# Group norm of an RWKV-7 time mix, taken head pair by head pair: centring product in PSUM, variance spread by a ones block, inverse root by logarithm and exponential

## What is computed

```python
y = tm(ys)                                   # 16 heads of 64
mean = jnp.mean(y, axis=-1, keepdims=True)
var = jnp.mean(jnp.square(y - mean), axis=-1, keepdims=True)
yn = ((y - mean) * lax.rsqrt(var + GN_EPS)).reshape(bsz, t_len, D_MODEL)
yn = yn * ln_w.astype(f32) + ln_b.astype(f32)
o = ((yn + bonus.reshape(bsz, t_len, D_MODEL)) * g.astype(f32)).astype(h.dtype)
return o @ w_o, ...
```

## Time and profile before

| | us |
|---|---|
| median of 3 runs | 1508.48 (1508.26 to 1512.67) |
| the profiled execution, its own time | 1510.38 |
| its span from the first to the last instruction | 1508.4 |
| PE busy in it | 1429.3 (95%) |
| DVE, ACT, POOL busy | 872.7, 565.6, 32.0 |
| group norm, first product to first product of `w_o` | from 611.7 to 641.0 |

### The profile page before, as it was taken

One profiled execution on the slowest core, in us unless ns is written; L12 is line 12 of the kernel. 1 busy time (PEld: TensorE's weight loads), 2 busy tenths in 40 slices (PEclk: granted clock), 3 DMA queues, 4 the chain that ended last, 5 costly groups with the idle time before them and its releaser, 6 DMA issues.

```text
span 1508.4 us, 28845 instructions
## 1 busy us (share of the span) xinstructions
PE 1429.3 (95%) x11934; PEld 1379.3 (91%) x11934; DVE 872.7 (58%) x1290; ACT 565.6 (37%) x724; POOL 32.0 (2%) x44
## 2 busy tenths in 40 slices
PE   4999999688799999899999999999999999999997
PEld 4999999577598998399999999999999999999997
DVE  5555544866995323676555546555556877655544
ACT  4333323385343320244333334334333235334332
POOL 0000000300001000100000000000000000000000
PEclk9999999898898995699999999999999999999998
DMA  4443344222244000124343444443344443444342
GB/s 190 158 146 141 114 135 163 90 86 92 60 146 134 11 17 33 53 85 167 139 141 139 135 165 145 142 155 139 131 139 157 155 153 124 155 158 148 124 154 94
DMA packets 44221, 189.00 MB, mean 125 GB/s; under 512 B 15888, under 2 KB 17296, under 8 KB 28016
## 3 DMA queue, kind: packets, MB, share of 16 engines
q1 hardware_dynamic: 44144, 187.89, 36.0%
HBM read 182.65 MB, written 5.22 MB: 125 GB/s over the span
## 4 chain that ended last, share of the span: by engine, by line
PE 86%; DVE 6%; ACT 4%; issue 3%; POOL 1%; DMA 1%; SPq 0%; DVEq 0%; ACTq 0%
PE psum L329 46%; PE psum L361 21%; PE psum L790 4%; PE psum L497 4%; ACT w_hi L242 1%; PE psum L968 1%; PE psum L1033 1%; PE psum L1020 1%; PE psum L1017 1%; PE psum L951 1%; PE psum L937 1%; PE psum L998 1%; PE psum L925 1%; DVE w_lo L247 1%; DVE rstd L318 1%
## 5 line engine op out<-in xcount | busy, mean ns | idle before, releaser
L329 PE MATMUL psum<-x_hi,w_hi 128*128 128x322 f32 (+2 forms) x1600 | 501.9, 314 | 22.8 <-DVE x_lo L294 17.8
L247 DVE TENSOR_TENSOR w_lo<-w_raw,w_hi 128x2048 fp32r<-128x2048 f32 (+1 forms) x188 | 388.6, 2067 | 226.4 <-ACT w_hi L242 226.0
L329 PE MATMUL psum<-x_lo,w_hi 128*128 128x322 f32 (+2 forms) x1600 | 501.3, 313 | 0.0
L329 PE MATMUL psum<-x_hi,w_lo 128*128 128x322 f32 (+2 forms) x1600 | 499.9, 312 | 0.0
L242 ACT ACTIVATE w_hi<-w_raw 128x2048 fp32r<-128x2048 f32 (+1 forms) x188 | 325.9, 1733 | 460.1 <-PE psum L329 229.2
L329 PEld LDWEIGHTS psum<-x_hi,w_hi 128*128 128x128 f32 x1600 | 302.6, 189 | 25.6 <-issue 21.5
L329 PEld LDWEIGHTS psum<-x_hi,w_lo 128*128 128x128 f32 x1600 | 303.5, 190 | 0.0
L329 PEld LDWEIGHTS psum<-x_lo,w_hi 128*128 128x128 f32 x1600 | 303.1, 189 | 0.3
L361 PE MATMUL psum<-h_hi,w_hi 128*128 128x322 f32 (+2 forms) x704 | 219.8, 312 | 0.0
L361 PE MATMUL psum<-h_lo,w_hi 128*128 128x322 f32 (+2 forms) x704 | 219.7, 312 | 0.0
L361 PE MATMUL psum<-h_hi,w_lo 128*128 128x322 f32 (+2 forms) x704 | 219.5, 312 | 0.0
(11 more groups left out here) (192 smaller groups left out, 1449.5 us busy)
## 6 DMA issues: line engine op xcount, KB each, us to landing
w_raw<-in_gu SPq DMA_DIRECT2D x88, 1024.0 KB, 4.8
w_raw<-in_down SPq DMA_DIRECT2D x64, 704.0 KB, 4.0
w_raw<-in_mix SPq DMA_DIRECT2D x16, 1024.0 KB, 4.8
w_raw<-in_scin SPq DMA_DIRECT2D x12, 1024.0 KB, 4.8
w_raw<-in_wo SPq DMA_DIRECT2D x4, 1024.0 KB, 4.9
w_raw<-in_scout SPq DMA_DIRECT2D x4, 1024.0 KB, 4.7
s<-in_wkv SPq DMA_DIRECT2D x8, 256.0 KB, 4.4
out_wkvs<-s SPq DMA_DIRECT2D x8, 256.0 KB, 2.0
```

The costliest lines, as they stand in the source:

```text
L247: dve.tensor_tensor(wlo[par][:, :n], raw[par][:, :n], whi[par][:, :n].bitcast(F32), ALU.subtract).then_inc(lo_ready, 1)
L329: last = pe.matmul(PS[:, banks[j], :n], w[:, (2 * k + j) * P:(2 * k + j + 1) * P], v[:, k, :n], start=(k == 0 and i == 0), stop=(k == KT - ...
```

## The change

The group norm is done pair by pair, with other operations:

- A matrix `centre` (one on the diagonal minus a 64th of the head's block of ones) is built once, on DVE, after the inverses. PE multiplies y by it (L890 of the new kernel; this is the centred y) into PSUM banks 4 to 7, and it stays there. DVE's subtraction is gone.
- ACT squares it out of PSUM. PE multiplies the squares by the block of ones into banks 2 and 3, so the sum stands on all 64 rows of the head: the pass that spread it is gone.
- ACT takes the logarithm of the variance plus epsilon, and then the exponential of minus one half of it: the inverse root. Square root and reciprocal are gone.
- DVE multiplies the centred y in PSUM by the inverse root in memory. DVE also writes the low part of the result, which POOL did.
- PE starts the group norm only when the last state and the last bonus have left banks 4 to 7 (`seq_ready`, `bonus_ready`). Before, its first two passes used banks 0, 1 and 6.
- `seq_stored` is split in two; DVE waits for the four stores whose memory it takes, SP for the other four before it loads slot 2 of `w_o`.

```diff
             pe.wait_ge(y_evac, CHUNKS)
-            for p in range(PAIRS):
+            pe.wait_ge(centre_ready, 1)
+            pe.wait_ge(seq_ready, SEQS)
+            pe.wait_ge(bonus_ready, PAIRS)
+
+            def centred(p):
+                if p >= 4:
+                    pe.wait_ge(gn_used, p - 3)
+                pe.matmul(PS[:, 4 + p % 4, :NY], centre[:, :], ar[:, 1, p, YC:], start=True, stop=True)\
+                    .then_inc(yc_ready, 1)
+
+            def variance(p):
+                pe.wait_ge(yc_sq, p + 1)
                 if p >= 2:
-                    pe.wait_ge(yc_ready, p - 1)
-                pe.matmul(PS[:, p % 2, :NY], con[:, K_BLOCK:K_BLOCK + P], ar[:, 1, p, YC:], start=True, stop=True)\
-                    .then_inc(mean_done, 1)
...
+                    pe.wait_ge(gn_log, p - 1)
+                pe.matmul(PS[:, 2 + p % 2, :NY], con[:, K_BLOCK:K_BLOCK + P], tmp[6 + p % 2][:, :NY],
+                          start=True, stop=True).then_inc(var_done, 1)
+
+            for p in range(4):
+                centred(p)
+            variance(0)
+            variance(1)
+            for p in range(2, PAIRS):
+                variance(p)
+                if p + 2 < PAIRS:
+                    centred(p + 2)
             project_pe(pe, "wo", 2, T - 14, 0)
...
+            def square(p):
                 act.wait_ge(yc_ready, p + 1)
                 if p >= 2:
                     act.wait_ge(var_done, p - 1)
-                act.activation(tmp[6 + p % 2][:, :NY], ar[:, 1, p, YC:], ACT.Square).then_inc(yc_sq, 1)
...
+                act.activation(tmp[6 + p % 2][:, :NY], PS[:, 4 + p % 4, :NY], ACT.Square).then_inc(yc_sq, 1)
+
+            def inverse_root(p):
+                root = (acc, ms)[p % 2][:, :NY]
+                act.wait_ge(var_done, p + 1)
+                if p >= 2:
+                    act.wait_ge(gn_used, p - 1)
+                act.activation(root, PS[:, 2 + p % 2, :NY], ACT.Ln, bias=GN_EPS, scale=1.0 / HD).then_inc(gn_log, 1)
+                act.wait_ge(gn_log, p + 1)
+                act.activation(root, root, ACT.Exp, scale=-0.5).then_inc(gn_inv, 1)
+
+            def take_o(p):
                 act.wait_ge(o_ready, p + 1)
                 act.activation(ohi[:, p, :NY], tmp[2 + p % 4][:, :NY], ACT.Copy).then_inc(ohi_ready, 1)
+
+            square(0)
+            square(1)
+            for p in range(PAIRS):
+                inverse_root(p)
+                if p + 2 < PAIRS:
+                    square(p + 2)
+                if p:
+                    take_o(p - 1)
+            take_o(PAIRS - 1)
             project_act(act, "wo", 2)
...
             inverses(dve, split)
+            link(dve, dve.tensor_scalar(centre[:, :], con[:, K_BLOCK:K_BLOCK + P], -1.0 / HD, None, ALU.mult))
+            for hh in range(2):
+                rows = slice(HD * hh, HD * hh + HD)
+                last = dve.tensor_tensor(centre[rows, rows], centre[rows, rows], con[rows, K_EYE:K_EYE + HD], ALU.add)
+            last.then_inc(centre_ready, 1)
             split(16)
             chain_dve(dve, split)
...
-                dve.tensor_tensor(t, PS[:, 4 + p % 2, :NY], ar[:, 1, p, YC:], ALU.mult).then_inc(gn_used, 1)
+                dve.wait_ge(gn_inv, p + 1)
+                dve.tensor_tensor(t, PS[:, 4 + p % 4, :NY], (acc, ms)[p % 2][:, :NY], ALU.mult).then_inc(gn_used, 1)
                 dve.wait_ge(gn_used, p + 1)
...
+                if p:
+                    low_o(p - 1)
+            low_o(PAIRS - 1)
             project_dve(dve, "wo", 2)
```

More of the change, by code:

```diff
@@ L146, in build_program @@
         one = at("one", [P, C], start=o4 + 4 * PAIRS * (PCHUNKS + SEQS) + 4 * T)
+        centre = at("centre", [P, P], start=o4 + 4 * PAIRS * (PCHUNKS + SEQS) + 4 * T + 4 * C)
         gt = [at("gt0", [P, C * C], start=iv), at("gt1", [P, C * C], start=e_start + 6 * 4 * TS)]
@@ L736, in build_program @@
         seq_ready = sem("seq_ready")
-        seq_stored = sem("seq_stored")
+        seq_stored = [sem(f"seq_stored{i}") for i in range(2)]
         final_stored = sem("final_stored")
@@ L881, in mix_pe @@
             pe.wait_ge(y_evac, CHUNKS)
[L882 to L896 removed]
+            pe.wait_ge(centre_ready, 1)
[8 more added lines that the diff above has]
+                pe.wait_ge(yc_sq, p + 1)
+                if p >= 2:
+                    pe.wait_ge(gn_log, p - 1)
[9 more added lines that the diff above has]
+                    centred(p + 2)
             project_pe(pe, "wo", 2, T - 14, 0)
[L899 removed]
+        centre_ready = sem("centre_ready")
         rk_spread = sem("rk_spread")
@@ L1275, in mix_pool @@
                 last.then_inc(arm_ready, 1)
-            for p in range(PAIRS):
-                pool.wait_ge(ohi_ready, p + 1)
-                pool.tensor_tensor(olo[:, p, :NY], tmp[2 + p % 4][:, :NY], ohi[:, p, :NY].bitcast(F32),
-                                   ALU.subtract).then_inc(olo_ready, 1)
         def inverses(dve, split):
@@ L1448, in mix_dve, with low_o @@
             inverses(dve, split)
+            link(dve, dve.tensor_scalar(centre[:, :], con[:, K_BLOCK:K_BLOCK + P], -1.0 / HD, None, ALU.mult))
[3 more added lines that the diff above has]
+            last.then_inc(centre_ready, 1)
             split(16)
             chain_dve(dve, split)
-            for p in range(PAIRS):
-                dve.wait_ge(mean_done, p + 1)
-                dve.scalar_tensor_tensor(out=ar[:, 1, p, YC:], in0=PS[:, p % 2, :NY], scalar=-1.0 / HD, in1=ar[:, 1, p, YC:],
-                                         op0=ALU.mult, op1=ALU.add).then_inc(yc_ready, 1)
-            dve.wait_ge(gn_root, 1)
-            dve.reciprocal(rstd[0:HEADS, :NY], ms[0:HEADS, :NY]).then_inc(gn_inv, 1)
-            dve.wait_ge(seq_stored, 16 * SEQS)
+            def low_o(p):
+                dve.wait_ge(ohi_ready, p + 1)
+                dve.tensor_tensor(olo[:, p, :NY], tmp[2 + p % 4][:, :NY], ohi[:, p, :NY].bitcast(F32),
+                                  ALU.subtract).then_inc(olo_ready, 1)
+            dve.wait_ge(seq_stored[0], 16 * SPC)
+            dve.wait_ge(bonus_ready, PAIRS)
             for p in range(PAIRS):
```

15 lines of the change are left out of this document (3 added, 12 removed).

## The result

| | before | after |
|---|---|---|
| median in one comparison | 1510.27 (6 runs, 1508.26 to 1512.83) | 1517.62 (6 runs, 1516.39 to 1522.87) |
| ratio after to before | | 1.0054, interval 1.0039 to 1.0069: +8.2 us (5.9 to 10.4) |
| profiled execution, its span | 1508.4 | 1514.4 |

The forecast of 1512.4 and its range to 1516.0 were both too low. The ratio and its interval are estimated from all runs of a comparison and are not the quotient of the medians, which lie 7.35 us apart. The kernel after was timed twice more, beside the experiments: 1.0055 (1.0037 to 1.0073) and 1.0052 (1.0033 to 1.0072). Slower it is: the medians of the three comparisons lie 7.35, 8.5 and 6.9 us apart.

The account below looks back on a forecast made before the run. PE was taken as the bound, waiting on the serial group norm, with ACT's table loads pacing the new one. The first projection slot's end moved from 649.39 to 653.35, so 1508.5 + 3.9 = 1512.4, range 1510.0 to 1516.0.

Parts of the forecast that it names:

- 1 PE's start: Group norm's first product on PE: waits for the last bonus, at 612.42 instead of 611.74, 0.7 us lost.
- 2, 3 first logarithm: Four centring products end at 616.7; with 1.2 us for the first variance product, ACT's first logarithm starts at 617.9.
- 4 first exponential: On ACT, logarithm 0.44 and table load 1.28 with small gaps: the first exponential starts at 619.65.
- 5 first to last exponential: ACT's pair loop with two table loads: five steps of 4.28 us and two of 3.92, together 29.2.
- 6 last gate operation ends: DVE's multiply, weight and bonus, bias and gate on the last pair: ends at 651.05.
- rival D: ACT's steps slightly shorter or the clock rising early: 0.3 us back in step 3, total 1512.1; within the forecast's width.
- rival B: Table loads cost nothing after the first: first projection slot 8.5 us earlier, total 1500.0; chance 0.05.
- rival C: Each table switch hides a 1.38 us drain on ACT: 20.7 us on top of 3.9, total 1533; chance 0.03.
- step 7: Projection's first slot: after the last low parts, PE's 12 products of tiles 6 and 7 take 1.8 us, ending at 653.35.
- Rival A: Clock falls after PE's pause before tile 6: 12 products take 3.3 us, slot end +5.4, total 1514.1; chance 0.30.
- everything behind it as before, shifted: After the projection's first slot, the program's end moves by as much as that slot's end, nothing added.
- same: Whole program within the 4.5 us (0.3%) that a measurement can tell, line at 1513.0; chance 0.51.

Follow-up runs that it names:

- b_exp: Kernel before plus a one-element exponential right after the group norm's square root; 1511.6, ratio 1.0006.
- b_wait: Kernel before plus the changed kernel's wait of PE for the last state and last bonus before the group norm; 1512.51, ratio 1.0008.
- a_sqrt: Changed kernel plus a one-element square root on ACT after the last high part; 1514.32, ratio 1.0025.
- a_copy: Changed kernel with the logarithm replaced by a copy, for timing only, the computed result being different; 1500.83, ratio 0.9939.
- a_fill_more: Changed kernel plus twelve unused products in PE's pause before tile 6 of the output projection, repeated in more rounds; 1515.86, ratio 1.0051.
- a_pool: Kernel of a_abs with the low parts moved from DVE back to POOL; 1496.10, ratio 0.9919.
- a_abs: Changed kernel with one inverse-root function for logarithm and exponential, plus a one-element square root after the last high part; 1495.24, ratio 0.9908.

## Why the prediction was wrong, point by point

The terms of the stage, counted from PE's first product in the forecast (612.42) and in the trace (609.98):

| step | forecast | measured |
|---|---|---|
| 1 PE's start, against before | +0.7 | +0.78 |
| 2, 3 first logarithm | 5.48 | 5.74 |
| 4 first exponential | 7.23 | 7.49 |
| 5 first to last exponential | 29.2 | 28.87 |
| 6 last gate operation ends | 38.63 | 38.61 |
| 7 tile 6 starts | 39.13 | 39.07 |
| 7 the 12 products of tiles 6 and 7 | 1.8 | 2.57 |

In the second execution of the kernel after everything from the first logarithm to tile 6 came 0.8 earlier (tile 6 at 38.30), in the third as in the table; rival D had said that the clock may rise early, and gave it 0.3.

**Right.** Every load took 1.28 and none was free (against rival B) or had anything hidden behind it (against rival C). The exponentials stand 4.22 apart for 4.28, since the high part starts 0.32 behind the square (630.15 to 630.47) where I took 0.36. DVE's gate operation took 0.55 to 0.56 throughout. DVE waited for ACT 1.8 to 2.2 us in a pair. `centre` took 0.22 + 0.45 on DVE ahead of a weight's low part, and the wait on `seq_stored` ended nothing: DVE's first multiplication was released by the exponential (the wait of 8.2 us for L1227, the longest).

```profile
464.08 0.22 DVE L1473 TENSOR_SCALAR centre<-con 128x128 f32<-128x128 f32 x1
464.34 0.45 DVE L1476 TENSOR_TENSOR centre<-centre,con 64x64 f32<-64x64 f32 x2
464.82 2.71 DVE L248 TENSOR_TENSOR w_lo<-w_raw,w_hi 128x2048 fp32r<-128x2048 f32 x1
```

**Wrong: step 7, "At 2.4 GHz they take 12 x 0.15".** Rival A was what happened, in all three executions. It gave +5.4 for the slot's end and +5.6 in the time. The trace has 0.78 + 3.99 = 4.8 at the slot's end and 0.78 + 4.84 = 5.6 at the next stage (second execution 4.8, third 5.6): its price was about right, its chance of 0.30 too small. The fall itself costs 1.4 to 1.5 us, as the filled pause shows; in the two executions with the pause filled the next stage came 3.4 and 3.7 later than before, close to the forecast's 3.9. What misled me was the earlier trace rows, where the clock stayed at 1.00 behind a pause of PE. I read it as what such a pause does. It was one outcome of two. The same pause, in the same place of the last channel mixing, ended otherwise in the profiled execution of the kernel after. First before, then after (columns: stretch, length, PE's busy time, clock, DMA share, GB/s):

```profile
1160.00:1163.00 3.00, 1.22 (x9) 1.00 0.00 0
...
1165.00:1168.00 3.00, 3.00 (x22) 1.00 0.73 306
```

```profile
1165.00:1168.00 3.00, 1.02 (x7) 1.00 0.00 0
1168.00:1170.00 2.00, 2.00 (x12) 0.72 0.48 127
1170.00:1172.00 2.00, 2.00 (x9) 0.50 0.96 397
```

In 8 of the 13 profiled executions the clock fell behind this pause, in 5 it did not, and the stretch from the 145th product of the stage behind the time mix to the end of the program then measures 816.7 instead of 815.2. b_exp and b_wait, both edits of the kernel before, are among the eight; a_sqrt, a_copy, a_fill_more and a_pool, all edits of the kernel after, among the five. It is 2 of 3 executions with the old arrangement and 6 of 10 with the new one, so nothing ties these 1.5 us to the change; all three of the kernel after itself fell, the one of the kernel before did not, and that is too few to exclude a share. I count them to the spread between executions, which I had read as 0.3% of noise without asking what made it.

**Wrong: "everything behind it as before, shifted".** This term was put at nothing, and no rival had it; the runs show 1.43 us. The range had room for the slow tail, and not for this and a higher median besides: rival A's 1514.1 and 1.43 make 1515.5, and with the 1.8 of the next paragraph 1517.3, beside the measured 1517.62. The root of the next norm had its table from the old group norm. The earlier trace rows showed two loads at the root's place and I asked of each only what it costs, not who lives on it afterwards. Behind the sixteen loads of the new list stands a seventeenth, at L315, 1.43 us on PE's path. The order of ACT's list shows it in front of L315, where the list of before has none; a_sqrt and b_exp show the price from both sides.

**The median I started from.** 1508.48 came from three runs. The later comparisons have 1510.27, 1510.80, 1510.08 and 1509.28 for the same kernel. So 1.8 us of the distance between 1512.4 and 1517.62 lie in the start, about 3.4 in the change: 7.35 between the medians where the forecast had 3.9. Of that the tail explains 0.8, the second slot's low clock 0.85 and the missing table 1.43, together 3.1; the sum of all stretches is 7.05 (above), within the interval 5.9 to 10.4. The 0.3 left are below what these times can tell. Two slips of the prediction are as small: 653.35 - 649.39 is 3.96 and not 3.9, and its own terms add up to chances of 0.49 for "same" and 0.44 for "slower", where it has 0.51 and 0.42.

**Where the expected gain went.** The new arrangement is better by itself: with one inverse root for logarithm and exponential (and the root's table given back) it is worth 13 to 14 us. The two functions of different tables in each pair take 16.7 us (a_copy) to 17.9 (a_abs) at the first slot's end, and that is more than it brings. The Trainium skill, "ScalarE: Activation LUTs", section "Table sets: the hidden batching unit", says that one set holds both functions and that a logarithm followed by an exponential needs one load. The trace has a load of 1.28 before every one of the sixteen. The kernel's source names no loads and no sets, and whether one set for both can be had here was not tried; it is the open way to keep logarithm and exponential.

## What to carry to other kernels

A table load has two prices: its own 1.28 us, and that of the load which the next user of the evicted table then needs; follow the engine's list to the next function with a table, however far behind, and put a one-element call of it where the engine is idle. Operations that alternate between two tables cost two loads each time, so group them or find one function for both, before counting what else the new arrangement saves. A clock that stays up behind a pause in one trace is one outcome; look for the same pause in other executions before building on it. Filling it kept the clock up in both tries, though no gain in the time was shown.

## What the hardware showed that I had not expected

- The same pause of PE, 1.98 us in the same place, was followed by a fall of the clock in 8 executions and not in 5. The fall came 0.1 to 1.6 us behind PE's first product after the pause, and cost 1.5 us each time.
- The time at which one core's program reaches the group norm spreads by 9 us (608.0 to 617.1), with the same instructions ahead of it but for the build of `centre`; the same kernel alone spread by 4.9.
- ACT's `Abs_reciprocal_sqrt` on 322 columns out of PSUM took 0.42 to 0.45 us, as the logarithm (0.44) and the square (0.42 to 0.46) did. One load of 1.28 served all eight, the squares and copies between them included.
